# Down biases moved into the first block's product, one slot table on two column tiles, and constant matmuls in three router waits

## The chip, the cores and the metric

One core of a Trainium2 chip runs the whole kernel. The metric is the device time of one execution in microseconds (us); lower is better. The kernel before takes 1793.83 us (median of 3 runs, 1792.36 to 1794.33).

## What is computed

One inference step of a layer: an mLSTM branch and a latent-attention branch, merged, an output projection and a residual (x1), then an RMSNorm (x2) and a mixture of experts with top 4 of 32, then the final norm. Everything is float32. There are 336 tokens (64 of the sample stream, 272 of the prompt stream) of width 1024. Cut to what the change touches:

```python
logits = x2 @ w_router + b_router
top_v, top_i = lax.top_k(logits, TOP_K)
gates = softmax(top_v)
# sort (token, expert) pairs by expert, pad each expert's rows to whole blocks
ys = block of rows: hid @ w_dn[e] + b_dn[e],   hid = (up + 1) * gate * sigmoid(1.702 * gate)
x = x1 + sum over the token's experts of ys * gate
```

## The kernel before, in words

The kernel is written for each engine by hand: each engine has its own program, and they meet by semaphores. Eight PSUM banks are handed out in the order of a list of jobs (`job_list`, from L143): job n has bank n modulo 8, and `begin` (L578), `filled` and `taken` wait by that number.
**Up to the router.** Projections, attention and mLSTM run first. Then the output projection makes x1 in three row tiles (128, 128 and 80 tokens), each is normed into x2, transposed (`x2_turned`), copied by ScalarE and multiplied by the router's weights (`router`), and VectorE finds the top 4 (`choose`). `count(t)` (L895 to L902) counts the chosen experts with matmuls of constants.

**The tables.** VectorE works out for each of the 336 x 4 pairs a slot in padded blocks of 64 rows (BLK): the block `blkc` and the slot in it, `slotc`, for 12 columns of 128 rows. `inblk` (12 x 55, one-hot over the blocks) and `inslot` (12 x 64, one-hot over the slots) are factors of a matmul that scatters values into a table of 64 slots by 55 blocks. Two values are scattered: the token (`valc`, multiplied into the left half of `spread` by GpSimd at L1805) and the row of the result (`val4`: four times the token plus the turn, which of the token's up to four experts this is; right half, by VectorE). So job `tab` is 12 matmuls of 110 columns into partitions 0 to 63, and job `tab2` is the same 12 again into partitions 64 to 127, for the indices of the second half of each result row. VectorE reads `tab` with one operation (add and minimum) into `idxf`, casts it to `idx` (semaphore `idx_set`), and GpSimd gathers the 64 token rows of block 0 by it (`rows_in`, L1810). Before job `tab` TensorE waits for `tab_d` (VectorE, `inslot` and the right half of `spread`) and `tab_p` (GpSimd's half). `moe_tab` says that the tables of all engines are ready; PE then reads the number of blocks into a register.

**Down biases.** The sum over experts of gate times b_down is one matmul of K = 32: `gateT` (32 x tokens) by `bd_rows` (32 x 1024), six matmuls of 512 columns (`down_bias`, L934): two (tile t = 0, jobs `bd`) stand before the first block's tokens are transposed, four (t = 1, 2) behind the gate and up product of block 0. VectorE adds each to x1.

**Blocks.** For each of 39 blocks: 64 gathered rows are transposed (`tokens_turned`) and copied by ScalarE to `xg`; `bias` adds gate and up biases (L965); `gate_up(k)` for k = 0 to 7 (L975, and L981 for k = 7) multiplies with two column tiles of 64 (the halves of a bank), 1 MB of weights for each k; VectorE and ScalarE make `hid`; `hidden_turned`; `down(j)` (L998). Block 0's `gate_up` stands before the loop; the loop's pass b does the down product of block b and the `gate_up` of block b + 1. The order is: tokens, bias, hidden turn, gate_up(0), down(0), down(1), down(2), gate_up(1), down(3), gate_up(2) to (7).

**Weights.** The on-chip ring holds one expert's 12 MB (12 loads of 1 MB). SyncE (L545 to L553) reloads a slot for the next expert when TensorE has gone over it for the last block of the expert that was there: eight gate/up loads wait for `m_up`, then four down loads for `m_down`, one after another in its queue. Expert 0's weights are loaded before the router.

Of the kernel before, what the change touches and what calls it, by code (L numbers as in the profile page):

```python
# [18 lines left out]
ALU = mybir.AluOpType  # L19
# [7 lines left out]
NT = TS + TP  # L27
# [8 lines left out]
NB1 = MAXB + 2  # L36
# [8 lines left out]
for _name, _n in [("ident", 128), ("ones", 128), ("below", 128), ("cos", NT), ("sin", NT), ("swap", 64),  # L45
                  ("mask", NT), ("sel", 4 * 128), ("expert", NE), ("block", NB1), ("lane", 1),
                  ("slot", BLK), ("thr", 6), ("tok", 12), ("pad", 3), ("tok4", 12)]:
    CONST_AT[_name] = (_at, _n)
    _at += _n
# [3 lines left out]
def constants():  # L53
    c = np.zeros((128, CONST_N), np.float32)

    def put(name, a):
        o, n = CONST_AT[name]
        c[:a.shape[0], o:o + n] = a

    put("ident", np.eye(128))  # L60
    put("ones", np.ones((128, 128)))
    put("below", np.triu(np.ones((128, 128)), 1))
    half = ROPE // 2
    pos = np.concatenate([TM + PAST + np.arange(TS), np.arange(TP)]).astype(np.float32)
# [20 lines left out]
    put("tok", first + p - NT)  # L85
    put("tok4", TOPK * (first + p - NT))
    put("pad", np.concatenate([NT + p % BLK, 2 * (TOPK * NT + p % BLK) + p // BLK,
                               np.where(p % BLK, 2 * NT, NT - 1)], axis=1))
    return c
# [36 lines left out]
def job_list():  # L126
# [40 lines left out]
    j += [("pos",), ("cntT",), ("x2T", 2, 0), ("x2T", 2, 1), ("lg", 2), ("pend",), ("tab",), ("be",), ("gT",), ("tab2",)]  # L167
    j += [("bd", 0, s) for s in range(2)]
    return j
# [12 lines left out]
def build(nc, i, o, x_rows_dram, y_rows_dram):  # L182
    with ExitStack() as ctx:
# [39 lines left out]
        def r3(ap, a):  # L223
            return ap.rearrange("p (a b) -> p a b", a=a)
# [76 lines left out]
        posm = r3(small(3 * NE), 3)  # L301
        slotc, blkc, valc = small(12), small(12), small(12)
        nblkT, pendT = small(1, NE), small(1, NE)
# [19 lines left out]
        inblk = r3(r_kv[:, 1536:1536 + 12 * NB1], 12)  # L323
        spread = r3(r_o[:, 384:384 + 24 * NB1], 12)
        prod = r_o[:, 0:384].rearrange("p (t k e) -> p t k e", t=3, k=4)
# [41 lines left out]
        def taken(eng, *name):  # L367
# [26 lines left out]
        x_sent, yrow_free = sem("x_sent"), sem("yrow_free")  # L394
        nblkT_set, cmpT_set, gates_norm, inblk_set, tab_d, tab_p, idx_set, table_clear, be_set, idx_now = map(sem, (
            "nblkT_set", "cmpT_set", "gates_norm", "inblk_set", "tab_d", "tab_p", "idx_set", "table_clear", "be_set",
            "idx_now"))
# [182 lines left out]
        def _(pe):  # L580
# [6 lines left out]
            def end(ins, *name):  # L587
                ins.then_inc(bank_full[JOB[name] % 8], 1)
# [302 lines left out]
            def count(t):  # L891
# [11 lines left out]
                if t == 2:  # L903
                    end(ins, "cntT")

            count(0)
            x2_turned(2)
            router(2)
# [3 lines left out]
            b = begin("pend")  # L912
            end(group(b[0:NE, 0:1], [(cst("below")[0:NE, 0:NE], nblkT[:, :])]), "pend")
            pe.wait_ge(tab_d, 1)
            pe.wait_ge(tab_p, 1)
            pairs = [(inslot[0:m, 4 * t + k, :], spread[0:m, 4 * t + k, :]) for t, (_, m) in enumerate(ROWS)
                     for k in range(4)]
            b = begin("tab")
            end(group(b[0:BLK, 0:2 * NB1], pairs), "tab")
            pe.wait_ge(cmpT_set, 1)  # L920
# [6 lines left out]
            end(ins, "gT")  # L927
            b = begin("tab2")
            end(group(b[BLK:2 * BLK, 0:2 * NB1], pairs), "tab2")
            taken(pe, "gT")  # L930

            def down_bias(b, t, s):
                c0, m = ROWS[t]
                return pe.matmul(b[0:m, :], gateT[:, c0:c0 + m], bd_rows[:, 512 * s:512 * s + 512], start=True, stop=True)  # L934

            for s in range(2):
                b = begin("bd", 0, s)
                end(down_bias(b, 0, s), "bd", 0, s)

# [8 lines left out]
            pe.wait_ge(moe_tab, 1)  # L949
            for name in ("pos", "cntT", "pend", "be", "tab", "gT", "tab2"):  # L950
                taken(pe, name)
            for s in range(2):
                taken(pe, "bd", 0, s)
            nb = pe.value_load(nbi[0:1, 0:1].bitcast(I32), min_val=NE, max_val=MAXB)
            pe.wait_ge(m_xrow, 16)
            tokens_turned()
# [366 lines left out]
        def _(dve):  # L1323
# [302 lines left out]
            for t in range(3):  # L1626
# [23 lines left out]
            step(stt(slotc, blkc, -float(BLK), d12, ALU.mult, ALU.add))  # L1650
            step(tt(valc, cst("tok"), slotc, ALU.subtract))
            signal(tt(inblk, cst("block").unsqueeze(1).broadcast_to([128, 12, NB1]),
                      blkc.unsqueeze(2).broadcast_to([128, 12, NB1]), ALU.is_equal), inblk_set, 1)
            step(tt(later, dest.unsqueeze(3).broadcast_to([128, 3, 4, 4]), dest.unsqueeze(2).broadcast_to([128, 3, 4, 4]),
# [3 lines left out]
            step(tt(val4, val4, turn_of.rearrange("p t k -> p (t k)"), ALU.add))  # L1658
            step(tt(spread[:, :, NB1:2 * NB1], inblk, val4.unsqueeze(2).broadcast_to([128, 12, NB1]), ALU.mult))
            signal(tt(inslot, cst("slot").unsqueeze(1).broadcast_to([128, 12, BLK]),  # L1660
# [19 lines left out]
            signal(ts(pick, lane, be[:, 0:1], ALU.is_equal), m_pick, 1)  # L1680
            take(ts(idxf[0:BLK, 1, :], tab[0:BLK, NB1:2 * NB1], 2.0, ALU.mult, cst("pad", BLK)[:, 1:2], ALU.add), "tab")
            filled(dve, "tab2")
            take(ts(idxf[BLK:128, 1, :], bank(("tab2",))[BLK:128, NB1:2 * NB1], 2.0, ALU.mult,
                    cst("pad")[BLK:128, 1:2], ALU.add), "tab2")
            signal(dve.tensor_copy(idx[:, 1, :].bitcast(U32), idxf[:, 1, :]), idx_set, 2)
            for s in range(2):
                filled(dve, "bd", 0, s)
                x = x1[:, 0, 512 * s:512 * s + 512]
# [69 lines left out]
        def _(pool):  # L1758
# [46 lines left out]
            pool.tensor_tensor(spread[:, :, 0:NB1], inblk, valc.unsqueeze(2).broadcast_to([128, 12, NB1]), ALU.mult  # L1805
                               ).then_inc(tab_p, 1)

            def rows_in(column):
# [69 lines left out]
```

## Time and profile before

| what | us |
|---|---|
| median of 3 runs | 1793.83 |
| the profiled execution's own time | 1794.13 |
| its span | 1792.3 |
| TensorE busy | 1596.8 (89%) |
| VectorE busy | 363.6 (20%) |
| ScalarE busy | 372.3 (21%) |
| GpSimd busy | 122.1 (7%) |
| HBM read | 471.26 MB, 272 GB/s over the span |

The span is what the trace covers; about 1.8 us of the execution's own time lie outside it. Busy time of TensorE is modelled from its pipelined instructions. Times in rows are counted from the span's start. The router and its tables lie at about 640 to 698 us, block 0 begins at 698 us, and the blocks last to some 30 us before the end.

### The profile page before, as it was taken

Reading aid. Unit: us, or ns where it says so; the run is one execution under the profiler, and the core shown is the slowest. Engines: PE = TensorE matmul, PEld = TensorE weight load, DVE = VectorE, ACT = ScalarE, POOL = GpSimd, SP = SyncE. Lnnn points to the kernel's source line nnn. Section 1 sums busy time; section 2 is a strip of 40 time slices with the busy share of each in tenths; the row PEclk is TensorE's granted clock in tenths of the full one; section 3 lists DMA queues with packets and bytes.
Section 4 is the critical chain, followed back from the end, with each engine's and each line's share of the span. In section 5 each row is a group of like instructions: output and inputs, shape, how many; then the busy total and the mean of one; then the engine's idle time right before and its main releaser. Section 6 shows DMA issues by size and latency. Waiting matters only on the chain.

```text
span 1792.3 us, 20636 instructions
## 1 busy us (share of the span) xinstructions
PE 1596.8 (89%) x7124; PEld 732.7 (41%) x7125; DVE 363.6 (20%) x859; ACT 372.3 (21%) x724; POOL 122.1 (7%) x219
## 2 busy tenths in 40 slices
PE   6899999999999997988879998878899978899894
PEld 4565665666666643322223332222233322233231
DVE  3443442223231123110101101100111100111015
ACT  3443242353430020110101111101111101111111
POOL 0100000000000000100001010100011100011000
PEclk9989999899999997998989999989899989899997
DMA  7212112221209524899998999999999999849898
GB/s 251 69 47 74 47 48 94 72 71 47 95 1 303 187 99 175 347 409 413 413 405 324 401 354 413 411 409 407 362 363 360 405 409 406 351 179 406 339 403 283
DMA packets 108777, 477.36 MB, mean 266 GB/s; under 512 B 12995, under 2 KB 16944, under 8 KB 75970
## 3 DMA queue, kind: packets, MB, share of 16 engines
q1 hardware_dynamic: 100696, 461.77, 65.9%
q0 software_dynamic: 7808, 15.00, 2.5%
q8 instruction: 23, 0.38, 0.1%
q10 hardware_dynamic: 234, 0.08, 0.0%
q14 instruction: 16, 0.13, 0.0%
HBM read 471.26 MB, written 15.50 MB: 272 GB/s over the span
## 4 chain that ended last, share of the span: by engine, by line
PE 70%; DMA 17%; DVE 5%; issue 3%; SPq 2%; ACT 1%; DVEq 0%; ACTq 0%; POOL 0%; POOLq 0%
PE bank L592 30%; PE bank L975 20%; DMA ring<-in_w_gate_up 16%; PE bank L998 16%; PE bank L596 3%; PE bank L981 1%; DVE r_kv L1346 1%; DVE r_v L1349 1%; DMA b_router_b<-in_b_router 1%; SPq L546 0%; SPq L553 0%; SPq L462 0%; DVE r_c L1349 0%; DVE r_qk L1343 0%; DVE ring L1343 0%
## 5 line engine op out<-in xcount | busy, mean ns | idle before, releaser
L975 PE MATMUL bank<-ring,r_kv 128*64 128x512 f32 x2184 | 521.1, 625 | 95.6 <-DMA ring<-in_w_gate_up 95.6
L975 PEld LDWEIGHTS bank<-ring,r_kv 128*64 128x64 f32 x2184 | 157.1, 142 | 408.7 <-issue 309.0
L998 PE MATMUL bank<-ring,r_kv 128*64 128x512 f32 x1248 | 294.6, 616 | 0.7 <-ACT r_kv L1063 0.7
L592 PE MATMUL bank<-r_xt,ring 128*128 128x336 f32 x848 | 256.6, 458 | 1.8 <-DVE r_xt L1346 1.5
L1343 DVE TENSOR_SCALAR r_kv<-bank 128x512 f32<-128x512 f32 (+1 forms) x80 | 54.9, 687 | 930.5 <-PE bank L981 924.0
L592 PEld LDWEIGHTS bank<-r_xt,ring 128*128 128x128 f32 x848 | 161.7, 194 | 83.4 <-issue 13.2
L998 PEld LDWEIGHTS bank<-ring,r_kv 128*64 128x64 f32 x1248 | 93.8, 145 | 200.6 <-issue 199.7
L1063 ACT ACTIVATE r_xt<-bank 128x512 f32<-128x512 f32 x39 | 23.3, 597 | 521.6 <-PE bank L998 521.6
L592 PE MATMUL bank<-ring 128*128 128x336 f32 (+4 forms) x336 | 98.2, 435 | 4.1 <-DVE ring L1502 3.9
L1289 ACT ACTIVATE r_o<-r_kv 128x512 f32<-128x512 f32 x39 | 24.6, 632 | 324.7 <-DVE r_kv L1343 324.7
L596 PEld LDWEIGHTS bank<-const,r_v 64*128 64x128 f32 (+3 forms) x524 | 45.4, 139 | 79.4 <-DVE r_v L1349 44.5
L592 PEld LDWEIGHTS bank<-ring 128*128 128x128 f32 (+4 forms) x336 | 59.1, 184 | 39.5 <-issue 16.8
L592 PE MATMUL bank<-ring,r_kv 128*128 128x128 f32 (+6 forms) x256 | 72.5, 417 | 2.1 <-DVE r_kv L1346 1.2
L981 PE MATMUL bank<-ring,r_kv 128*64 128x512 f32 x312 | 73.5, 592 | 0.0
L596 PE MATMUL bank<-const,r_v 64*128 64x64 f32 (+3 forms) x524 | 61.8, 255 | 12.1 <-DVE r_v L1349 10.2
L1063 ACT ACTIVATE r_kv<-bank 128x512 f32<-128x512 f32 (+3 forms) x85 | 49.8, 586 | 80.8 <-PE bank L596 75.9
L592 PE MATMUL bank<-r_kv,ring 128*128 128x336 f32 (+10 forms) x240 | 59.5, 379 | 0.0
L965 PE MATMUL bank<-bgu,r_qk 32*64 32x512 f32 x312 | 44.2, 636 | 12.0 <-DVE r_kv L1343 12.0
L592 PEld LDWEIGHTS bank<-ring,r_kv 128*128 128x128 f32 (+4 forms) x256 | 40.1, 189 | 33.9 <-issue 24.7
L1289 ACT ACT_TABLE_LOAD x39 | 50.0, 1283 | 12.7 <-ACT r_xt L1063 12.6
L1834 POOL COPY r_qk<-r_qk 128x1 uint32 x39 | 7.0, 180 | 570.2 <-ACT r_xt L1063 570.2
L592 PEld LDWEIGHTS bank<-r_kv,ring 128*128 128x128 f32 (+3 forms) x240 | 35.5, 179 | 24.1 <-issue 14.3
(235 smaller groups left out, 988.2 us busy)
## 6 DMA issues: line engine op xcount, KB each, us to landing
ring<-in_w_gate_up SPq DMA_DIRECT2D x256, 1024.0 KB, 17.1
ring<-in_w_down SPq DMA_DIRECT2D x128, 1024.0 KB, 14.6
ring<-in_w_in SPq DMA_DIRECT2D x12, 2048.0 KB, 8.1
ring<-in_w_proj_b SPq DMA_DIRECT2D x2, 2048.0 KB, 8.8
ring<-in_w_proj_a SPq DMA_DIRECT2D x2, 2048.0 KB, 8.9
ring<-in_w_out SPq DMA_DIRECT2D x2, 2048.0 KB, 7.8
ring<-y_rows SPq DMA_DIRECT2D x8, 512.0 KB, 9.1
ring<-in_w_uq SPq DMA_DIRECT2D x2, 1152.0 KB, 9.0
```

The source lines that it names most:

```text
L592: ins = pe.matmul(out, l, r, start=(n == 0), stop=(n == len(pairs) - 1), **kw)
L596: return pe.transpose(out, src, ident[0:src.shape[0], 0:src.shape[0]])
L965: pe.matmul(half(gate_bank if q < 2 else up_bank, q % 2), pick[32 * q:32 * q + 32, :], bgu[32 * q:32 * q + 32, :], start=True, stop=False, ...
L975: ins = pe.matmul(half(gate_bank if q < 2 else up_bank, q % 2), xg[:, k, :], w[:, 512 * q:512 * q + 512], start=False, stop=False, skip_gr ...
L981: ins = pe.matmul(half(bank_, t), xg[:, 7, :], w[:, 512 * (q0 + t):512 * (q0 + t) + 512], start=False, stop=True, skip_group_check=True)
L998: ins = pe.matmul(half(out_bank, t), hidT[:, j, BLK * h:BLK * h + BLK], w[:, h, 512 * t:512 * t + 512], start=(j == 0 and h == 0), stop=(j ...
L1063: return act.activation(out, src, ACT.Copy, scale=scale)
L1289: act.activation(sg, gt, ACT.Sigmoid, scale=ALPHA).then_inc(m_sig, 1)
L1343: return dve.tensor_scalar(out, a, s1, s2, op0, op1)
L1346: return dve.tensor_tensor(out, a, b, op)
L1349: return dve.scalar_tensor_tensor(out=out, in0=a, scalar=s, in1=b, op0=op0, op1=op1)
L1834: pool.tensor_copy(now[:, 1:2].bitcast(U32), idx[:, 1, bass.ds(pool.snap(b), 1)].bitcast(U32)).then_inc(idx_now, 1)
```

## The change

- `count(0)` is followed by two matmuls of constants of 512 columns (`keep_going`), `pend` by five, and the read of the number of blocks by one. Their results are overwritten.
- One table in place of two: `spread` has 55 columns for each of 12, the token's half (`valc`, constant `tok`, GpSimd's multiply, semaphores `inblk_set` and `tab_p`) is gone. Job `tab` is now 12 x 2 matmuls of 55 columns, alternately into partitions 0 to 63 and 64 to 127; `tab2` is gone. The token is worked out from the combined value by two more `ts` operations (add, times 0.25; add, add a large constant; subtract it, minimum), and one operation makes the result rows of both halves.
- The two matmuls of jobs `bd` and their waits are gone from in front of block 0. All six down biases stand within block 0's `gate_up`: four before k = 2, two before k = 5 (these wait until VectorE has added the first two). The loop waits for all six.

```diff
-    j += [..., ("pend",), ("tab",), ("be",), ("gT",), ("tab2",)]
-    j += [("bd", 0, s) for s in range(2)]
+    j += [..., ("pend",), ("tab",), ("be",), ("gT",)]
...
+            def keep_going(b, n):
+                for _ in range(n):
+                    pe.matmul(b[:, :], ident, const[:, 0:512], start=True, stop=True, skip_group_check=True)
             count(0)
+            keep_going(begin("x2T", 2, 0), 2)
             x2_turned(2)
...
             end(group(b[0:NE, 0:1], [(cst("below")[0:NE, 0:NE], nblkT[:, :])]), "pend")
+            keep_going(begin("tab"), 5)
             pe.wait_ge(tab_d, 1)
-            pe.wait_ge(tab_p, 1)
...
-            end(group(b[0:BLK, 0:2 * NB1], pairs), "tab")
+            for n, (l, r) in enumerate(pairs):
+                for half_ in range(2):
+                    ins = pe.matmul(b[BLK * half_:BLK * half_ + BLK, 0:NB1], l, r, start=(n == 0), ...)
+            end(ins, "tab")
...
-            b = begin("tab2")
-            end(group(b[BLK:2 * BLK, 0:2 * NB1], pairs), "tab2")
...
-            for s in range(2):
-                b = begin("bd", 0, s)
-                end(down_bias(b, 0, s), "bd", 0, s)
...
             nb = pe.value_load(nbi[0:1, 0:1].bitcast(I32), min_val=NE, max_val=MAXB)
+            keep_going(xt_bank, 1)
             pe.wait_ge(m_xrow, 16)
             tokens_turned()
...
             for k in range(8):
+                if k == 2:
+                    for n in range(4):
+                        down_bias(banks[4 + n], n // 2, n % 2).then_inc(bd_full, 1)
+                if k == 5:
+                    pe.wait_ge(bd_free, 2)
+                    for n in range(4, 6):
+                        down_bias(banks[n], n // 2, n % 2).then_inc(bd_full, 1)
                 gate_up(k, 0)
-            for n, (t, s) in enumerate([(t, s) for t in (1, 2) for s in range(2)]):
-                down_bias(banks[4 + n], t, s).then_inc(bd_full, 1)
-            pe.wait_ge(bd_free, 1)
+            pe.wait_ge(bd_free, 6)
...
-            step(tt(valc, cst("tok"), slotc, ALU.subtract))
...
-            step(tt(spread[:, :, NB1:2 * NB1], inblk, val4..., ALU.mult))
+            step(tt(spread, inblk, val4..., ALU.mult))
...
-            step(ts(idxf[0:BLK, 0, :], tab[0:BLK, 0:NB1], cst("pad", BLK)[:, 0:1], ALU.add, cst("pad", BLK)[:, 2:3],
-                    ALU.min))
+            step(ts(idxf[0:BLK, 0, :], tab[0:BLK, 0:NB1], cst("pad", BLK)[:, 0:1], ALU.add, 0.25, ALU.mult))
+            step(ts(idxf[0:BLK, 0, :], idxf[0:BLK, 0, :], -0.375, ALU.add, 12582912.0, ALU.add))
+            step(ts(idxf[0:BLK, 0, :], idxf[0:BLK, 0, :], 12582912.0, ALU.subtract, cst("pad", BLK)[:, 2:3], ALU.min))
...
-            take(ts(idxf[0:BLK, 1, :], ...), "tab")
-            filled(dve, "tab2")
-            take(ts(idxf[BLK:128, 1, :], ...), "tab2")
+            take(ts(idxf[:, 1, :], tab[:, 0:NB1], 2.0, ALU.mult, cst("pad")[:, 1:2], ALU.add), "tab")
...
-            for s in range(2):
-                filled(dve, "bd", 0, s)
-                take(tt(x, bank(("bd", 0, s))[:, :], x, ALU.add), "bd", 0, s)
-            for n, (t, s) in enumerate([(t, s) for t in (1, 2) for s in range(2)]):
+            for n in range(6):
+                t, s = n // 2, n % 2
...
-                signal(tt(x, banks[4 + n][0:m, :], x, ALU.add), bd_free, n + 1)
+                signal(tt(x, banks[4 + n % 4][0:m, :], x, ALU.add), bd_free, n + 1)
...
-            pool.wait_ge(inblk_set, 1)
-            pool.tensor_tensor(spread[:, :, 0:NB1], inblk, valc..., ALU.mult).then_inc(tab_p, 1)
```

## Rows read from the trace of the kernel before

**Rows 1.** The page: busy tenths of the DMA engines, 40 slices of 44.8 us.

```profile
DMA  7212112221209524899998999999999999849898
```

**Rows 2.** Chain that ended last, whole run: start us, us, what.

```profile
760.61 16.46 DMA ring<-in_w_gate_up
```

**Rows 3.** DMA stretches: us, busy us of five engines, PEclk, DMA share, GB/s.

```profile
703.00:722.00 19.00, 15.42 (x70) 5.35 (x70) 5.49 (x12) 1.11 (x2) 1.14 (x2) 0.90 0.98 410
...
724.00:730.00 6.00, 6.00 (x28) 1.96 (x28) 0.00 (x0) 0.60 (x1) 0.00 (x0) 0.91 0.12 34
```

**Rows 4.** Timeline of SyncE's queue, block 0 and after: start us, us, what.

```profile
701.66 12.33 SPq L549 DMA_DIRECT2D ring<-in_w_gate_up  x8
728.51 7.24 SPq L553 DMA_DIRECT2D ring<-in_w_down  x4
```

**Rows 5.** Chain that ended last, 679 to 749 us: start us, us, what.

```profile
679.27 0.18 DVE r_qk L1346
...
680.84 0.91 DVE r_qk L1346
...
688.86 2.42 PE bank L592 x24
...
694.00 0.99 issue
694.99 1.10 PE bank L596 x8
696.09 1.91 PE bank L965 x8
698.00 13.76 PE bank L975 x56
711.76 1.72 PE bank L981 x8
713.48 3.64 PE bank L934 x8
...
724.39 2.22 PE bank L975 x8
...
743.77 0.89 PE bank L981 x4
...
748.34 1.87 PE bank L975 x8
```

**Rows 6.** Stretches of the router and block 0: columns as in rows 3.

```profile
667.00:687.50 20.50, 9.89 (x58) 9.25 (x59) 14.59 (x47) 3.05 (x9) 1.85 (x2) 0.50 0.47 184
...
695.00:701.00 6.00, 6.00 (x24) 2.21 (x26) 0.00 (x0) 1.88 (x2) 0.95 (x1) 0.50 0.08 25
```

**Rows 7.** Timeline of TensorE, 656 to 688 us, start first; brackets: idle before.

```profile
656.60 7.03 PE L592 MATMUL bank<-ring,r_kv 128*80 128x512 f32 x16
663.47 1.87 PE L592 MATMUL bank<-r_xt,r_o 128*128 128x32 f32 x16
...
667.87 1.33 PE L596 MATMUL bank<-const,r_qk 80*128 80x80 f32 x8 [1.89 <-DVE r_qk L1349]
669.83 2.31 PE L592 MATMUL bank<-r_xt,r_o 128*80 128x32 f32 x16 [0.63 <-ACT r_o L1063]
...
675.73 0.26 PE L592 MATMUL bank<-r_qk,const 32*32 32x1 f32 x2 [0.52 <-DVE r_qk L1636]
683.88 4.23 PE L592 MATMUL bank<-r_o,r_kv 128*64 128x110 f32 x24 [7.88 <-DVE r_kv L1346]
```

**Rows 8.** Timeline, an mLSTM chunk's scores: 64 weight columns, 64 moving columns.

```profile
417.05 1.15 PE L592 MATMUL bank<-r_qk 128*64 128x64 f32 x16
```

**Rows 9.** Timeline, VectorE's first table read and GpSimd's first gather.

```profile
688.22 0.33 DVE L1343 TENSOR_SCALAR r_qk<-bank,const 64x55 f32<-64x55 f32 x1 [1.92 <-PE bank L592]
...
689.70 1.04 POOL L1810 DMA_INDIRECT r_v<-x_rows,r_qk  x1 [7.98 <-DVE r_qk L1677]
```

**Rows 10.** DMA issues from 680 to 705 us: median us from issue to landing.

```profile
r_v<-x_rows,r_qk POOLq DMA_INDIRECT x2, 3.2
```

More of the change, by code:

```diff
@@ L46 @@
                   ("mask", NT), ("sel", 4 * 128), ("expert", NE), ("block", NB1), ("lane", 1),
-                  ("slot", BLK), ("thr", 6), ("tok", 12), ("pad", 3), ("tok4", 12)]:
+                  ("slot", BLK), ("thr", 6), ("pad", 3), ("tok4", 12)]:
     CONST_AT[_name] = (_at, _n)
@@ L84, in constants @@
     first = np.repeat([c0 for c0, _ in ROWS], TOPK)[None, :]
-    put("tok", first + p - NT)
     put("tok4", TOPK * (first + p - NT))
-    put("pad", np.concatenate([NT + p % BLK, 2 * (TOPK * NT + p % BLK) + p // BLK,
+    put("pad", np.concatenate([TOPK * NT + p % BLK, 2 * (TOPK * NT + p % BLK) + p // BLK,
                                np.where(p % BLK, 2 * NT, NT - 1)], axis=1))
@@ L166, in job_list @@
         j += [("lg", t - 1)] if t else []
-    j += [("pos",), ("cntT",), ("x2T", 2, 0), ("x2T", 2, 1), ("lg", 2), ("pend",), ("tab",), ("be",), ("gT",), ("tab2",)]
-    j += [("bd", 0, s) for s in range(2)]
+    j += [("pos",), ("cntT",), ("x2T", 2, 0), ("x2T", 2, 1), ("lg", 2), ("pend",), ("tab",), ("be",), ("gT",)]
     return j
@@ L301, in build @@
         posm = r3(small(3 * NE), 3)
-        slotc, blkc, valc = small(12), small(12), small(12)
+        slotc, blkc = small(12), small(12)
         nblkT, pendT = small(1, NE), small(1, NE)
@@ L323, in build @@
         inblk = r3(r_kv[:, 1536:1536 + 12 * NB1], 12)
-        spread = r3(r_o[:, 384:384 + 24 * NB1], 12)
+        spread = r3(r_o[:, 384:384 + 12 * NB1], 12)
         prod = r_o[:, 0:384].rearrange("p (t k e) -> p t k e", t=3, k=4)
@@ L394, in build @@
         x_sent, yrow_free = sem("x_sent"), sem("yrow_free")
-        nblkT_set, cmpT_set, gates_norm, inblk_set, tab_d, tab_p, idx_set, table_clear, be_set, idx_now = map(sem, (
-            "nblkT_set", "cmpT_set", "gates_norm", "inblk_set", "tab_d", "tab_p", "idx_set", "table_clear", "be_set",
+        nblkT_set, cmpT_set, gates_norm, tab_d, idx_set, table_clear, be_set, idx_now = map(sem, (
+            "nblkT_set", "cmpT_set", "gates_norm", "tab_d", "idx_set", "table_clear", "be_set",
             "idx_now"))
@@ L918, in _ @@
             b = begin("tab")
-            end(group(b[0:BLK, 0:2 * NB1], pairs), "tab")
+            for n, (l, r) in enumerate(pairs):
+                for half_ in range(2):
+                    ins = pe.matmul(b[BLK * half_:BLK * half_ + BLK, 0:NB1], l, r, start=(n == 0), stop=(n == len(pairs) - 1),
+                                    skip_group_check=True)
+            end(ins, "tab")
             pe.wait_ge(cmpT_set, 1)
@@ L949, in _ @@
             pe.wait_ge(moe_tab, 1)
-            for name in ("pos", "cntT", "pend", "be", "tab", "gT", "tab2"):
+            for name in ("pos", "cntT", "pend", "be", "tab", "gT"):
                 taken(pe, name)
-            for s in range(2):
-                taken(pe, "bd", 0, s)
             nb = pe.value_load(nbi[0:1, 0:1].bitcast(I32), min_val=NE, max_val=MAXB)
+            keep_going(xt_bank, 1)
             pe.wait_ge(m_xrow, 16)
@@ L1650, in _ @@
             step(stt(slotc, blkc, -float(BLK), d12, ALU.mult, ALU.add))
-            step(tt(valc, cst("tok"), slotc, ALU.subtract))
-            signal(tt(inblk, cst("block").unsqueeze(1).broadcast_to([128, 12, NB1]),
-                      blkc.unsqueeze(2).broadcast_to([128, 12, NB1]), ALU.is_equal), inblk_set, 1)
+            step(tt(inblk, cst("block").unsqueeze(1).broadcast_to([128, 12, NB1]),
+                    blkc.unsqueeze(2).broadcast_to([128, 12, NB1]), ALU.is_equal))
             step(tt(later, dest.unsqueeze(3).broadcast_to([128, 3, 4, 4]), dest.unsqueeze(2).broadcast_to([128, 3, 4, 4]),
@@ L1658, in _ @@
             step(tt(val4, val4, turn_of.rearrange("p t k -> p (t k)"), ALU.add))
-            step(tt(spread[:, :, NB1:2 * NB1], inblk, val4.unsqueeze(2).broadcast_to([128, 12, NB1]), ALU.mult))
+            step(tt(spread, inblk, val4.unsqueeze(2).broadcast_to([128, 12, NB1]), ALU.mult))
             signal(tt(inslot, cst("slot").unsqueeze(1).broadcast_to([128, 12, BLK]),
@@ L1680, in _ @@
             signal(ts(pick, lane, be[:, 0:1], ALU.is_equal), m_pick, 1)
-            take(ts(idxf[0:BLK, 1, :], tab[0:BLK, NB1:2 * NB1], 2.0, ALU.mult, cst("pad", BLK)[:, 1:2], ALU.add), "tab")
-            filled(dve, "tab2")
-            take(ts(idxf[BLK:128, 1, :], bank(("tab2",))[BLK:128, NB1:2 * NB1], 2.0, ALU.mult,
-                    cst("pad")[BLK:128, 1:2], ALU.add), "tab2")
+            take(ts(idxf[:, 1, :], tab[:, 0:NB1], 2.0, ALU.mult, cst("pad")[:, 1:2], ALU.add), "tab")
             signal(dve.tensor_copy(idx[:, 1, :].bitcast(U32), idxf[:, 1, :]), idx_set, 2)
-            for s in range(2):
-                filled(dve, "bd", 0, s)
-                x = x1[:, 0, 512 * s:512 * s + 512]
-                take(tt(x, bank(("bd", 0, s))[:, :], x, ALU.add), "bd", 0, s)
-            for n, (t, s) in enumerate([(t, s) for t in (1, 2) for s in range(2)]):
+            for n in range(6):
+                t, s = n // 2, n % 2
                 m = ROWS[t][1]
@@ L1802, in _ @@
                 pool.dma_start(x_rows_dram[c0:c0 + m, :], x2[0:m, t, :]).then_inc(x_sent, 16)
-            pool.wait_ge(inblk_set, 1)
-            pool.tensor_tensor(spread[:, :, 0:NB1], inblk, valc.unsqueeze(2).broadcast_to([128, 12, NB1]), ALU.mult
-                               ).then_inc(tab_p, 1)
             def rows_in(column):
```

## The prediction, made before the changed kernel ran

> **What bounds the kernel now.** I read the page's slices first: the DMA engines are at 8 to 9 tenths almost everywhere from slice 17 on [rows 1], so the expert blocks live near the weight stream. The chain that ended last agrees: from 760.61 us it runs through a 16.5 us gate/up weight load, the first of many, with stretches of TensorE between them [rows 2]. So what shortens a block's arithmetic is worth little; what lets block 0, and with it the whole stream, start earlier is worth its full size. That needs a second look at where the stream begins. Expert 1's gate/up loads are issued from 701.66 us, behind block 0's own gate_up, and the DMA engines are full (0.98, 410 GB/s) from 703 to 722; then they are nearly idle (0.12) from 724 to 730, because the down loads are issued only at 728.51, when block 0's first down product is done [rows 3, 4]. After that they stay busy. The event that starts the steady stream is therefore block 0's down product: what comes before it on TensorE's path, at 640 to 728 us, is what the end hangs on.
>
> The third view is that path in order of time [rows 5]. A row is start, duration, engine. The reader sees three costs. First, serial small steps of VectorE up to the tables. Second, TensorE at its lower clock level: the granted clock is 0.50 (1.2 GHz) from 667 to 687.5, after short matmuls with waits between them, and again from 695 to 701, after the wait of 1.80 us before the tokens [rows 6]. Third, a hole around block 0's end: four down biases (713.48), and the next gate_up only at 724.39, where in the following block it begins 2.85 us after the last one's end (743.77 plus 1.72, to 748.34) [rows 5].
>
> **The change, step by step.** Durations are of the profiled execution (1794.13 us, 0.30 above the median of 1793.83); gains are differences, so I take them off the median.
>
> 1. *Two constant matmuls after count(0).* A 512-column matmul at the full clock (2.4 GHz) takes 0.86 us (8 of them from 656.60 to 663.47), so two take 1.72 and fit in the idle 1.89 before the transposes of tile 2 [rows 7]: cost 0, at most 0.2 if the clock drops within. If they hold the clock, the third router product costs 1.87 in place of 2.31 and the transposes about 0.2 less [rows 7]. I take 0.65 gained; bounds 0.2 lost, 1.0 gained (counts warm too).
>
> 2. *One table's VectorE work.* The 0.18 at 679.27 (`valc`) goes. The operation at 680.84 lasts 0.91 for the same 12 columns, while GpSimd multiplies [rows 5]; with GpSimd's operation gone it should be 0.18, so 0.73 more. Gain 0.9. GpSimd was not itself waited for; it is idle afterwards, and nothing else is late in its queue.
>
> 3. *Five constant matmuls after pend.* By 1 they start about 0.65 earlier than 676.0 [rows 7], at 675.35. At the full clock they take 4.3 us, at half 8.6. `tab_d` comes at 683.88 less 0.65 less 0.9, that is 682.3. They end between 679.65 and 683.95; with a rise of the clock midway, 682. Cost: I take 0.1, bounds 0 and 1.6.
>
> 4. *The table.* Before, the 24 instructions of 110 columns took 4.23 us, mostly at half clock, and tab2's 24 took 2.42 at full clock, 0.101 each [rows 5, 7]. Now 48 instructions of 55 columns. The nearest row is the score product (64 weight columns, 64 moving): 16 in about 1.1, 0.068 each [rows 8], so 48 take 3.2 without overlap. Bounds: 24 x 0.068 = 1.6 (halves entirely side by side) and 48 x 0.101 = 4.8. I take 2.9 and the full clock: gain 1.3. Column tiles do overlap here for 512 columns: 8 instructions of gate_up take 1.72 us, 0.215 each, where the 128-row form takes 0.43 [rows 5, 7]. The Trainium skill (TensorE: Matmul & The Clock Gate, Part 3: Packing small matmuls) says that matmuls whose outputs lie in different column groups run concurrently; by it alone the table would take 1.6 and the gain would be 1.3 more. tab2's 2.42 us lay ahead of the down biases, and goes with them.
>
> 5. *Index work.* Two more VectorE operations before the gather, at most 0.33 each (the PSUM form) [rows 9]; without PSUM I take 0.25 each: cost 0.5. Both sit before the cast that GpSimd waits for.
>    So the table ends at 688.1 - 0.65 - 0.9 + 0.1 - 1.3 = 685.35, and the gather, issued 1.6 behind it before (689.70), is issued 2.1 behind it: 687.45, and lands 3.0 later (median 3.2 of two issues, one under load [rows 10]): 690.5.
>
> 6. *What PE does meanwhile.* It waits for `moe_tab` and for VectorE to free the table: the ops from 688.22 on take about 2.4 with the added ones, so 687.8; 0.99 of issue and register read [rows 5]; then one constant matmul, 0.86 to 1.71: 689.7 to 690.5. It is ready as the gather lands; cost 0, at most 0.3. The tokens' transposes begin at 690.5 in place of 694.99: **gain 4.5** (steps 1 to 5 give 2.25; the other 2.25 are the two down biases and their VectorE adds, which held the bank and the register read although the gather had landed near 692.7).
>
> 7. *Clock at block 0.* Before, PE was at half clock up to 701.2; seven gate_ups took 13.76 in place of 7 x 1.72 = 12.04 [rows 5, 6], 1.7 lost. Now PE is busy without a gap from 688.8, some 6 us sooner, against a block start 4.5 sooner: about 0.4 of cold is left. **Gain 1.3**; bounds 0 and 3 (the transposes' 1.10 and the biases' 1.91 were cold too).
>
> 8. *Down biases in block 0.* Six at 0.86 are 5.16. They are K = 32 by 128 columns amid products of 128 by 64. Four of them took 3.64 us, 0.20 over 4 x 0.86, with one change of form [rows 5]; four changes now make some 0.45. So +5.6; the 3.64 at the end go. The hole: from 717.12 to 724.39 is 7.27, since VectorE first had to do four adds, three gate operations and a register read before it took gate and up. All that is now done during the product, so the hole is the next block's 2.85 [rows 5]. 5.6 - 3.64 - 4.42: **gain 2.5**. The next gate_up took 2.22 partly cold, 1.87 warm: **0.35**. The wait for two adds before k = 5 is covered: 0.7 us adds against three gate_ups. Refill: k = 2 to 7 free their slots later, so expert 1's loads stall about 2 us before k = 2 and end at about 719.6; the down loads are issued at 719.9. No loss, but the slack is thin.
>
> Sum: 4.5 + 1.3 + 2.5 + 0.35 = 8.65 us at block 0's first down product, carried to the end because the stream from there on is shifted as a whole. 1793.83 - 8.65 = **1785.2 us** (the profiled execution 1785.5).
>
> **Rivals.** (a) *More*: the halves overlap and the clock holds throughout: table 1.3 more, clock 1.7 more: 1782.2. For it, gate_up's overlap. Against it, the gaps of 2 us and more that still lie between the short matmuls. (b) *The constants do not hold the clock*, or the 48 instructions cost 0.101 each: 1.3 + 0.65 of clock and 1.9 of table go, and up to 1.5 for a late step 3; some of it: about 1788.7 (1787 to 1790.2). For it: two warm matmuls followed by a router of 32-column products, of the kind behind which the clock fell at 667. (c) *The gain does not reach the end*: expert 1's gate/up loads, held up by the moved biases, end at 719.6 against about 723 before, only 3.4 earlier; if the stream hangs on these, 1793.83 - 3.4 = 1790.4, and with a late table 1792. For it: the row of a nearly full DMA up to 722. Against it: the idle 6 us after it. (d) *Slower*: changing the tile costs time. The place is the table (47 changes of column tile) and block 0 (4 changes of form). At 0.23 us a change they cost 51 x 0.23 = 11.7 and the time is 8.65 less that, 1796.9; it decides from 0.17 us a change. Against it: gate_up changes the column tile at every second instruction and shows nothing, and the one change of form in the trace costs 0.20 with four matmuls around it [rows 5]. The Trainium skill (TensorEngine Tiling, Key Properties) says that a change of tiling mode drains TensorE, and a change of tile alone does not; by that rule block 0's four changes would cost and the table's 47 would not, which leaves this rival about 1 us and the forecast as it is. The trace's 0.20 agrees.
> That the change does not do what it says is (b).
>
> **Numbers.** About 0.2% (3.6 us) can be told from no change; 1790.2 is the bound. Forecast 0.56, (a) 0.12, (b) 0.15, (c) 0.13, (d) 0.04. Faster is forecast, (a) and (b): 0.83. Same is (c): 0.13. Slower is (d): 0.04. The range: down to (a) with 0.7 of spread between runs, 1781.5; up through (b) to 1789.7, leaving out (c) and (d).
>
> **What would show it.** Right: the table at 2.5 to 3.3 us for 48 instructions; the gather issued near 687.5; transposes near 690.5; block 0's gate_up (with six down biases) from about 693.5, its down product 8 to 9 us earlier; down loads of expert 1 issued near 720; the hole behind block 0 at about 3 us. Wrong, step by step: a granted clock of 0.5 through the first gate_ups (7); the table start after 683 (3); the down loads shifted by 8 but the end by 3 (c); table over 4.8 us (d).

## The result and the profile after

The changed kernel takes 1781.34 us (median of 4 executions, 1779.35 to 1782.65) against 1793.09 for the kernel before in the same rounds (4 executions): ratio 0.9932, 95% interval 0.9916 to 0.9948. It is 11.75 us faster where 8.65 was forecast, and lies 0.16 us under the range's lower end of 1781.5. The profiled execution took 1780.27 us with a span of 1778.4. One execution of all that follow, a slow one of the kernel with the biases alone (1922.31 us, granted clock 0.82 against 0.93 to 0.94 in the others of that kernel), stands in no comparison.

The chain of the kernel after, in order of time, from the first constants to the next block; start, duration, what. It answers to [rows 5].

```profile
665.76 1.91 PE bank L907 x4
...
669.25 1.32 PE bank L590 x16
...
685.45 2.88 DMA r_v<-x_rows,r_qk
...
688.37 1.11 PE bank L594 x8
689.49 1.91 PE bank L965 x8
691.40 4.96 PE bank L975 x16
696.36 3.62 PE bank L940 x8
699.98 5.30 PE bank L975 x24
705.28 1.87 PE bank L940 x4
707.15 3.58 PE bank L975 x16
710.74 0.88 PE bank L981 x4
...
715.29 1.87 PE bank L975 x8
717.16 5.15 PE bank L998 x24
```

The timeline of the same kernel, for what [rows 7] and [rows 9] showed of before:

```profile
674.06 6.03 PE L907 MATMUL bank<-const 128*128 128x512 f32 x10
...
681.09 1.61 PE L925 MATMUL bank<-r_o,r_kv 128*64 128x55 f32 x48 [0.99 <-DVE r_kv L1351]
...
682.63 0.42 PE L590 MATMUL bank<-r_qk,const 32*128 32x55 f32 x2
...
683.37 0.14 DVE L1673 CAST r_qk<-r_qk 1x1 int32<-1x1 f32 x1
...
683.54 0.27 DVE L1348 TENSOR_SCALAR r_qk<-bank,const 64x55 f32<-64x55 f32 x1
...
685.45 1.01 POOL L1805 DMA_INDIRECT r_v<-x_rows,r_qk  x1 [17.02 <-DVE r_qk L1682]
...
686.73 1.53 PE L907 MATMUL bank<-const 128*128 128x512 f32 x2 [3.28 <-issue]
```

Stretches of TensorE in it (us, busy us, granted clock, DMA share, GB/s), against [rows 6]:

```profile
667.00:673.90 6.90, 4.16 (x39) 0.98 1.01 382
...
683.40:686.70 3.30, 0.04 (x1) 1.00 0.00 0
686.70:688.40 1.70, 1.55 (x3) 0.68 0.22 65
688.40:694.70 6.30, 6.30 (x26) 0.54 0.08 23
694.70:700.00 5.30, 5.30 (x18) 1.00 0.76 260
```

And SyncE's queue: first down loads of expert 1, and the last loads before the end, against [rows 4]:

```profile
719.06 7.24 SPq L551 DMA_DIRECT2D ring<-in_w_down  x4
...
1742.77 19.87 SPq L563 DMA_DIRECT2D ring<-y_rows  x12
```

The reader sees four things. The clock stays full through the third router product (0.98) and the 48 table instructions take 1.54 us (681.09 to 682.63), but then VectorE is what is late: it reads the table only at 683.54, 0.91 behind its end, after its own small operations. TensorE stands idle for 3.28 us before the single constant; the clock falls behind that idle stretch, during the constant (0.68), and block 0 begins at half clock (0.54), as before. Block 0's first down product begins at 717.16 (before: 724.39 + 2.22 = 726.61), 9.45 us earlier, 0.23 of which was there already before the router. The profiled executions lie further apart than that, 1794.13 to 1780.27, or 13.86: the first down load is issued 9.45 us earlier and the last loads 13.76 earlier (the kernel before issues these at 1756.53):

```profile
1756.53 20.01 SPq L565 DMA_DIRECT2D ring<-y_rows  x12
```

So the loop was 4.3 us shorter in this one execution (1023.7 in place of 1028.0 us), with nothing in it changed. Whether that belongs to the change was the first question for the experiments. In what follows the distance from the first `count` matmul to the first down load is used: 63.34 us in the kernel before, 54.12 after, so 9.2 gained.

### The profile page after: what moved, and what is told of

The parts are those of the page before. It is cut to its first block, busy times and chain, and to the rows that moved or that the text cites. A ratio compares the mean times of both kernels' runs of the same rounds, so it can differ in the third digit from the quotient of the medians.

```text
span 1778.4 us, 20662 instructions
## 1 busy us (share of the span) xinstructions
PE 1592.5 (90%) x7140; PEld 727.7 (41%) x7141; DVE 363.0 (20%) x859; ACT 372.7 (21%) x724; POOL 121.2 (7%) x218
## 4 chain that ended last, share of the span: by engine, by line
PE 71%; DMA 17%; DVE 6%; issue 3%; SPq 1%; ACT 1%; DVEq 0%; POOLq 0%; POOL 0%; ACTq 0%
PE bank L590 30%; PE bank L975 20%; DMA ring<-in_w_gate_up 16%; PE bank L998 16%; PE bank L594 3%; PE bank L981 1%; DVE r_kv L1351 1%; DVE r_v L1354 1%; DVE ring L1348 0%; SPq L544 0%; SPq L551 0%; DMA ring<-in_x_prompt 0%; DVE r_qk L1348 0%; DVE r_c L1354 0%; PE bank L940 0%
## 5 line engine op out<-in xcount | busy, mean ns | idle before, releaser
L590 PEld LDWEIGHTS bank<-ring 128*128 128x128 f32 (+4 forms) x336 | 58.1, 181 | 38.7 <-issue 15.5
L594 PE MATMUL bank<-const,r_v 64*128 64x64 f32 (+3 forms) x524 | 61.4, 253 | 10.5 <-DVE r_v L1354 10.4
```

Source lines behind the costliest of these rows:

```text
L590: ins = pe.matmul(out, l, r, start=(n == 0), stop=(n == len(pairs) - 1), **kw)
L594: return pe.transpose(out, src, ident[0:src.shape[0], 0:src.shape[0]])
```

## Experiments

**The down biases alone.** On the kernel before:

```diff
-            for s in range(2):
-                b = begin("bd", 0, s)
-                end(down_bias(b, 0, s), "bd", 0, s)
...
+                if k == 2:
+                    for n in range(4): down_bias(...)
+                if k == 5:
+                    pe.wait_ge(bd_free, 2)
+                    for n in range(4, 6): down_bias(...)
...
```

> The kernel before with only the down biases moved (none before block 0, four before k = 2 and two before k = 5 of its gate_up). Theory (the steps' prices hold and the shift is carried to the end): the gather had landed near 692.7, so the tokens' transposes begin 2.0 to 2.3 us earlier (about 692.8), block 0's stretch from the first gate_up to the next is 2.2 to 2.7 shorter, the first down product begins 4.5 to 5 us earlier than 726.61, and the median falls by 4 to 6 us. Rival (the later slots of the ring set the end): median within 2 us of before. Rival (changes of the tile's form drain the array): the six biases take over 7 us together.

Its timeline:

```profile
689.74 1.04 POOL L1805 DMA_INDIRECT r_v<-x_rows,r_qk  x1 [8.01 <-DVE r_qk L1675]
...
692.73 0.70 PE L595 MATMUL bank<-const,r_v 64*128 64x64 f32 x8 [1.42 <-DMA r_v<-x_rows,r_qk]
693.36 1.09 PE L958 MATMUL bank<-bgu,r_qk 32*64 32x512 f32 x8
```

The transposes now begin when the gather lands, at 692.73, as forecast. The distance to the first down load is 57.24 us, 6.1 less, of which 1.3 is luck with the clock (transposes and bias at full clock, 1.65 us in place of 2.94). The six biases take 5.5 us. The median of nine executions is 1788.85 against 1792.08 (27 executions), 3.2 us; the ratio, 0.9994 with 0.9975 to 1.0012, can't be told from no change. So the 4 to 6 us expected at the end are not shown, although the profiled execution itself was 5.9 us shorter than that of before. The difference is not explained; the nine executions range over 10.5 us.

**No constants.** `keep_going` emits nothing.

```diff
-                for _ in range(n):
+                for _ in range(0):
```

> The changed kernel without any of its eight constant matmuls; what is computed is the same. Theory (the first two hold the clock through the third router product, the five hold it for the table, the last one buys nothing because the clock fell before it): the clock falls after count(0) as before, the router product takes 2.2 to 2.4 in place of 1.32, the count and table follow at half clock, the table's 48 instructions take 3.0 to 3.3 in place of 1.61, and the gather is issued 2.5 to 3.5 us later than in the changed kernel (its read no longer waits for VectorE); block 0's own stretch is unchanged within 0.5. Median 2 to 4 us above the changed kernel. Rival (the clock would have held anyway or the constants cost what they give): within 1 us.

```profile
669.30 2.31 PE L590 MATMUL bank<-r_xt,r_o 128*80 128x32 f32 x16 [0.63 <-ACT r_o L1068]
...
682.45 2.81 PE L925 MATMUL bank<-r_o,r_kv 128*64 128x55 f32 x48 [6.99 <-issue]
...
697.18 3.70 PE L940 MATMUL bank<-r_v,r_o 32*128 32x512 f32 x8
700.81 7.01 PE L975 MATMUL bank<-ring,r_kv 128*64 128x512 f32 x24
```

The router product is back at 2.31 and the table at 2.81 us, both at half clock (the table a little cheaper than the 3.0 expected), and the distance to the first gather rises from 20.51 to 22.66 us, 2.15 later, less than the 2.5 to 3.5 expected. To the first down load it is 56.98 (54.12 with the constants): they are worth 2.9 us there. Median 1786.46, ratio 0.9970 (0.9956 to 0.9983) to before. The first two and the five together did their work; no kernel left out only one of the groups, so how the gain divides between them is not shown. A surprise is the last row: 24 gate/up instructions behind the four biases took 7.01 us, where the changed kernel took 5.37 in the same view.

**A delay of known size.**

```diff
             pe.wait_ge(m_xrow, 16)
+            keep_going(xt_bank, 8)
             tokens_turned()
```

> The changed kernel with eight more constant matmuls between the landing of the gather and the transposes of block 0's tokens. They take 8 to 11 us there, and the clock is full when block 0 begins, which gives back 2.5 to 3: the first down product comes 5 to 8 us later than in the changed kernel. Theory (all after it is shifted as a whole): the median is later by the shift of the profile's first down product, within 2 us. Rival (part of the start's gain is lost or enlarged later): the end moves by less than two thirds or by more than four thirds of it.

```profile
686.85 9.87 PE L907 MATMUL bank<-const 128*128 128x512 f32 x18 [3.24 <-issue]
```

The distance to the first down load is 59.56, 5.4 more than in the changed kernel (with block 0 at full clock, the 16 instructions in 3.65 us). The median is 1787.97, ratio 0.9981 (0.9963 to 0.9998) to before: 4.1 us gained where the distance says 3.8. Against all executions of the changed kernel (1782.65, below) it is 5.3 later, where the distance says 5.4. What starts later ends later by as much, as far as medians can tell: the interval is 6 us wide.

**The table's halves in turn.**

```diff
-            for n, (l, r) in enumerate(pairs):
-                for half_ in range(2):
+            for half_ in range(2):
+                for n, (l, r) in enumerate(pairs):
```

> The changed kernel with the table's 24 matmuls in another order: twelve for partitions 0 to 63, then twelve for 64 to 127. Theory (adjacent matmuls on different column tiles run side by side): without neighbours the 48 instructions take 3.0 to 3.3 us (0.068 each, as in the score product) in place of 1.61, but VectorE is late to read the table by 0.9, so the gather is issued only 0.6 to 0.9 us later; median within 1.5 us of the changed kernel. Rival (55 columns are simply cheap, 0.034 each in any order): 1.6 us again.

```profile
674.94 2.82 PE L925 MATMUL bank<-r_o,r_kv 128*64 128x55 f32 x48 [0.95 <-DVE r_kv L1351]
...
681.01 1.88 PE L907 MATMUL bank<-const 128*128 128x512 f32 x2 [2.51 <-issue]
...
683.87 1.44 PE L965 MATMUL bank<-bgu,r_qk 32*64 32x512 f32 x8
...
685.25 3.65 PE L975 MATMUL bank<-ring,r_kv 128*64 128x512 f32 x16
```

and TensorE's stretch behind the idle one (us, busy us, granted clock, DMA share, GB/s):

```profile
681.00:683.87 2.87, 2.85 (x10) 0.54 0.15 39
```

(This execution's router lies 6 us earlier in its span; only distances are compared.) The same 48 instructions take 2.75 us (2.82 less the last one's tail) in place of 1.54: neighbours on different column tiles run side by side (whether it is the matmuls or the weight loads of one tile beside the other's matmul, this doesn't separate). In turn, each costs 0.057, below the 0.068 of the score product [rows 8] and so below the 3.0 to 3.3 us expected. The gather is issued 0.46 us later. Yet the distance to the first down load is 52.80, 1.3 *less*: TensorE's idle stretch became 2.5 us in place of 3.3, and the clock, which fell behind it here too (0.54), was full again when block 0's gate_ups began (16 instructions in 3.65). Median 1781.12 against 1792.08, ratio 0.9937 (0.9917 to 0.9957). That pointed to the idle stretch.

**The changed kernel again, twice,** on two chips.

> The changed kernel again, unaltered, on the chip of the next three. Theory (the gain is 9 to 10 us up to block 0's first down product, and what the clock does before block 0 and in the waits for weights adds or takes some us, differently in each execution): median 9 to 12 us below the kernel before; from the third count to the first gate_up the same times within 0.1, except where the granted clock differs. Rival (the loop itself became shorter): from the first down product to the last loads, it is again 4 us shorter than in the kernel before.

> The changed kernel a third time, for the spread. Theory (9.2 us gained up to the first down load, and the loop as long as before): median 8 to 11 us below the kernel before; expert 1's first down load 54.1 us behind the first count at half clock before block 0, up to 2.9 less where the clock holds. Rival (11.75 us, as first measured, is its gain): median 11 to 13 us below.

SyncE's queue in the first of the two, then in the second:

```profile
720.94 7.24 SPq L551 DMA_DIRECT2D ring<-in_w_down  x4
...
1748.05 20.36 SPq L563 DMA_DIRECT2D ring<-y_rows  x12
```

```profile
718.22 7.24 SPq L551 DMA_DIRECT2D ring<-in_w_down  x4
...
1745.02 20.65 SPq L563 DMA_DIRECT2D ring<-y_rows  x12
```

The distance to the first down load is 54.10 and 54.14 us, the same to 0.04, while the loop takes 1027.1 and 1026.8 us, close to the 1028.0 of before. The shorter loop of the first profile does not come from the change. The length of the loop varies from execution to execution: 1023.7 to 1028.0 us over the fourteen profiles of all kernels, and 1027.1 and 1023.8 in two of one and the same kernel (wait filled and VectorE's order, below).

Medians: 1783.01 against 1791.85 (ratio 0.9946, 0.9931 to 0.9961; 8.8 us, just under the 9 to 12 expected) and 1782.71 against 1791.00 (0.9946, 0.9925 to 0.9967). Over all 17 executions of the changed kernel the median is 1782.65, over 54 of the kernel before 1792.08: **9.4 us gained**, beside the trace's 9.2.

**The idle stretch filled.**

```diff
             end(ins, "gT")
+            taken(pe, "cntT")
+            keep_going(bank(("cntT",)), 3)
             taken(pe, "gT")
```

> The changed kernel with three more constant matmuls, in the idle stretch between the gate transposes and the wait for the tables (their result is overwritten). Theory (block 0 began at half clock because TensorE stood idle for 3.3 us there): the clock stays full, the tokens' transposes, the bias and the first 16 gate/up instructions take 0.7, 0.9 to 1.1 and 3.4 to 3.65 in place of 1.11, 1.98 and 5.03, the first down product comes 2.5 to 3 us earlier relative to the gather's issue, and the median is 1 to 3 us below the changed kernel's. Rival (it was the waits after the register read): the clock still falls.

```profile
688.56 0.71 PE L594 MATMUL bank<-const,r_v 64*128 64x64 f32 x8 [0.70 <-DMA r_v<-x_rows,r_qk]
689.20 1.09 PE L967 MATMUL bank<-bgu,r_qk 32*64 32x512 f32 x8
690.21 3.65 PE L977 MATMUL bank<-ring,r_kv 128*64 128x512 f32 x16
693.80 3.69 PE L942 MATMUL bank<-r_v,r_o 32*128 32x512 f32 x8
697.42 7.07 PE L977 MATMUL bank<-ring,r_kv 128*64 128x512 f32 x24
```

and its stretches (us, busy us, granted clock):

```profile
686.00:690.00 4.00, 2.67 (x19) 1.00 0.10 28
693.80:697.40 3.60, 3.60 (x10) 1.00 0.88 355
697.40:701.00 3.60, 3.60 (x11) 0.53 0.50 205
```

Tokens, bias and the first gate_ups run at full clock, as expected. In all five profiles of kernels with the wait filled, block 0's first gate_ups ran at full clock; in all four profiles of the changed kernel, with and without its third constant, 16 instructions took 5.03 to 5.07. But the distance to the first down load falls by 0.85 only (53.27), not by 2.5 to 3, since the clock drops right behind the four down biases: TensorE was busy for 3.60 of 3.60 us there. Median 1781.90, ratio 0.9942 (0.9928 to 0.9955).

**VectorE's order as well.** In the kernel with the wait filled, the three operations on the block numbers go behind the cast that the gather waits for.

> The kernel of the filled wait, and VectorE's three small operations on the block numbers (0.56 us) behind the cast of the gather's indices instead of ahead of the table's read. Theory (VectorE, not the table, now ends last before the gather): the gather is issued 0.5 to 0.6 us earlier after the table's start (3.8 in place of 4.36), the tokens' transposes likewise unless TensorE is late from its constants; median 0 to 1 us below the filled wait alone. Rival (GpSimd or TensorE's register read ends last): nothing moves.

> The kernel of the filled wait and VectorE's order again, beside the changed kernel on one chip. Theory: table start, gather and tokens at the same distances from the first count as in its first profile (16.14, 19.91, 22.80 us); expert 1's first down load 50.8 us behind the first count, or up to 52.6 where the clock falls behind the four biases; median 1 to 4 us below the changed kernel's. Rival (its lower median was the spread between runs): less than 1 us below.

In the first of the two:

```profile
695.11 5.37 PE L977 MATMUL bank<-ring,r_kv 128*64 128x512 f32 x24
```

The gather is issued 19.91 and 19.93 us behind the first count in place of 20.51, and the first down load 50.81 and 50.85, 3.3 less than in the changed kernel; in both profiles the clock held behind the biases (24 instructions in 5.37 us), which alone is 1.7 of the 2.4 us by which they lie below the filled wait. The tokens came 0.7 earlier, which is the order's part. So the median lies 2.7 below the filled wait's, where 0 to 1 was expected. Medians 1779.17 (ratio 0.9926, 0.9907 to 0.9946) and 1779.35 (0.9933, 0.9910 to 0.9956). On the same chips the changed kernel had 1783.01 and 1782.71: this version is 3.8 and 3.4 us below it by the medians, though the intervals against the kernel before overlap. Its two medians are the lowest of all that ran.

**Without the third constant.** The line `keep_going(xt_bank, 1)` is left out.

> The changed kernel without the one constant matmul before the gather's wait. Theory (the clock has fallen before it; it only fills part of a wait): the tokens' transposes begin at the same time after the gather's issue (2.9 us), and the clock rises later in block 0, so that block 0's first gate/up stretch is 0 to 1 us longer. One time, within the spread of the changed kernel's. Rival (it holds the clock): block 0 is over 1.5 us longer.

Gather, transposes, first gate_ups and first down load lie at 20.51, 23.45, 26.41 and 54.15 us behind the first count, as in the changed kernel (20.51, 23.43, 26.39, 54.12). The third constant is worth nothing. Its one time was 1785.20.

**More down biases in a row.** To see whether the biases themselves let the clock go, the four before k = 2 are computed twice, in the kernel with the wait filled and VectorE's order.

```diff
+                    for n in range(4):
+                        down_bias(banks[4 + n], n // 2, n % 2)
                     for n in range(4):
                         down_bias(banks[4 + n], n // 2, n % 2).then_inc(bd_full, 1)
```

> The same kernel with four and two, and the four biases before k = 2 computed twice over (the first results are overwritten by equal ones), eight K = 32 matmuls in a row. Theory (such a run does not keep the clock): the granted clock falls to 0.5 within or right behind the eight, so that they and the next 24 gate/up instructions take 1.7 us or more over 6.9 + 5.2 = 12.1 us. Rival (TensorE fully busy holds the clock, and the falls seen came from the waits before block 0): 12.1 to 12.5 us and a clock of 1.0 throughout.

Its timeline, then its stretches:

```profile
692.90 9.74 PE L942 MATMUL bank<-r_v,r_o 32*128 32x512 f32 x16
702.56 7.80 PE L977 MATMUL bank<-ring,r_kv 128*64 128x512 f32 x24
```

```profile
694.00:696.00 2.00, 2.00 (x6) 1.00 1.02 422
...
698.00:700.00 2.00, 2.00 (x4) 0.50 0.12 49
```

Expected were 12.1 us for the two if the clock held; they took 17.4. The clock fell in the middle of the run, with TensorE busy all the time. In the delay kernel nine constants of 128 rows took 9.87 us in a row and ended at full clock (1.00 from 692.00 to 696.60, 4.60 of 4.60 us busy); eight biases of 32 rows began at full clock and ended at half. That points to these matmuls themselves. What in them it is, the 32 rows or the values they multiply, is not separated. The weight loads ran during the first half of them (DMA share 1.02) and not during the constants, but with the biases apart, below, they ran at 0.88 to 0.94 and the clock held. The one time was 1788.64.

**The biases apart,** in the same kernel.

```diff
-                if k == 2: ... four ...
-                if k == 5: ... two ...
+                if 1 <= k <= 6:
+                    n = k - 1
+                    if n == 4:
+                        pe.wait_ge(bd_free, 2)
+                    down_bias(banks[4 + n % 4], n // 2, n % 2).then_inc(bd_full, 1)
```

> The kernel of the filled wait and VectorE's order, with the six down biases one by one before k = 1 to 6 of block 0's gate_up in place of four and two together. Theory (a run of K = 32 matmuls can let the clock fall although TensorE is fully busy, as behind the four biases in the filled-wait kernel and in the one without constants; one between two gate_ups cannot): the granted clock stays at 1.0 through block 0, whatever the alignment; from the first gate_up to the first load of expert 1's down weights is 26.3 to 27.3 us (each change of form may add 0.05 to 0.2, twelve of them in place of four). Median within 2 us of the kernel with four and two. Rival (the fall had another cause): the clock falls again behind a bias in this or a like kernel.

```profile
686.26 1.94 PE L977 MATMUL bank<-ring,r_kv 128*64 128x512 f32 x8
688.13 1.12 PE L942 MATMUL bank<-r_v,r_o 32*128 32x512 f32 x2
```

The clock stays full through block 0, but eight more changes of form cost 1.35 us (the first down load at 52.20 in place of 50.85), 0.17 each; from the first gate_up it is 27.7 us, over the 26.3 to 27.3 expected. Median 1780.80, ratio 0.9939 (0.9915 to 0.9962); beside 1779.35 for four and two. Whether it is safer over many executions than four and two can't be told from one profile each.

The distances and the medians, side by side (us; gains against the kernel before, each on its own chip):

| kernel | to first down load | gained there | gained by the medians |
|---|---|---|---|
| before | 63.34 | | |
| changed (three times) | 54.12, 54.10, 54.14 | 9.2 | 11.75, 8.8, 8.3 |
| biases only | 57.24 | 6.1 | 3.2 |
| no constants | 56.98 | 6.4 | 5.6 |
| delay | 59.56 | 3.8 | 4.1 |
| halves in turn | 52.80 | 10.5 | 11.0 |
| filled wait | 53.27 | 10.1 | 10.0 |
| filled wait and order (twice) | 50.81, 50.85 | 12.5 | 12.7, 11.7 |
| biases apart | 52.20 | 11.1 | 10.2 |

Within 1 us, but for the first profile's kernel and the biases alone, what is gained up to the first down load is gained at the end.

## Why the prediction was right and wrong

**The bound: right.** Block 0's first down product sets when the weight stream runs steadily, and its shift is carried to the end, as the delay and the table of distances show; the biases alone are the exception, unexplained. Rival (c) is out: expert 1's gate/up loads did wait before k = 2 (their issue stretched over 18.12 us, 12.33 before), and nothing came of it.

**The range: wrong.** It ended 0.16 us above the measured median. The forecast was 1785.2; the 3.84 us between the two are made up of three parts. The three executions of before that I had (1793.83) lay 1.75 over the median of 54 (1792.08). The four of the changed kernel lay 1.31 under the median of 17 (1782.65). And the change gains 9.43 where the sum had 8.65: 0.78. The step that failed is the last of the numbers, the 0.7 us that I allowed for the spread between runs: single executions of the kernel before range over 15.8 us and medians of four to seven of the changed kernel over 1.7. In the first two traces the loop alone differed by 4.3 us. The lower end was rival (a)'s 1782.2 less that 0.7; the median of the 17, 1782.65, lies inside the range. What put 1781.34 outside is the spread, and not the mechanism.

**The sum, term by term** (by the profiles, 0.23 that lay before the router taken off):
- Step 1, first two constants: 0.65 forecast, 1.6 measured where VectorE compares the counts. The third router product took 1.32 us, not 1.87: I had taken the price of a product with 128 weight columns for one with 80, and the last counts ran at full clock too. Mis-sized.
- Step 2: 0.9 forecast, 0.94 measured. Step 3: the five constants ended at 680.1, 0.99 before `tab_d`; cost 0. Right.
- Step 4, the table: 2.9 us forecast, 1.54 measured, a little under the lower bound of 1.6. The step mis-sized is the overlap of the two column tiles, which I took as slight; the Trainium skill's rule (TensorE: Matmul & The Clock Gate, Part 3: Packing small matmuls) gave 1.6, and the trace agrees with its 1.54; the halves in turn show that it is the overlap. But of the 2.6 us gained only some 1.9 reached the gather, since VectorE read the table 0.9 behind its end (0.2 before). I had left that engine's order out.
- Step 5: 0.5 forecast, 0.43 measured; issue to landing 2.88 (3.0). So the gather is issued 4.0 us earlier, where steps 1 to 5 had 2.25. Step 6: from its issue to the tokens 2.4 us less than before, 2.25 forecast. Tokens: 4.5 us earlier forecast, 6.4 measured.
- Step 7, the clock at block 0: 1.3 forecast, nothing measured: the eight gate_ups together took 15.6 us, 15.5 before. The first 16 gate/up instructions took 4.96 us, in all four profiles of that part of the kernel 5.03 to 5.07 by the timeline, against 3.65 at full clock. I had TensorE busy from 688.8 on and did not count the 3.3 idle before that, behind which the clock fell. Filling them gave it back. The step's own figures also leave more cold than it says: with TensorE busy 6.2 us sooner and block 0 4.5 sooner, 1.5 of the 3.2 us at half clock remain and cost 0.75 us, not 0.4.
- Step 8: 2.5 forecast, 2.6 measured; six biases 5.49 (5.6), hole 2.83 (2.85). The gate_up behind it: 0.35 forecast and measured. Right.

So 1.9 us more than forecast up to the tokens and 1.3 us less in steps 7 and 8 nearly cancel, and that is luck: 9.2 against 8.65.

**The rivals.** (a) was half right: the halves overlap, the clock did not hold throughout; the version with the wait filled and VectorE's order, in which it did, is what (a) described. (b) is refuted by the kernel without constants for the first seven constants taken together, and holds for the eighth. (d) is out: 47 changes of column tile cost nothing measurable, and a change of form 0.17 each.

## What to carry to other kernels

Look for the event that starts the steady stream, measure variants by the distance of two events around the changed part in one trace, and use the median only to see that the distance is carried: here the distance repeated within 0.04 us and medians within 2. When a step is shortened, write down what every other engine still has to do at that point, because the next wait is often an engine that was hidden (VectorE here). Matmuls of constants pay where they bridge a wait right in front of work that is on the path, and one that comes only behind the idle stretch bought nothing here (54.15 us without it, 54.12 with it).

## What the runs showed of the hardware that was not expected

- TensorE can be busy without a gap and still lose its clock: behind or within a run of K = 32, 128-column matmuls the granted clock went from 1.0 to 0.5, with 3.60 of 3.60 us busy before it in one kernel, and in the middle of eight such matmuls in another, while a run of nine constants with 128 rows rose from half clock and ended at full clock. With four in a row before k = 2 it fell in two of eleven profiles.
- Adjacent matmuls of 55 columns on the two column tiles cost 0.032 us an instruction, and 0.057 when the tiles are not alternated, both at full clock (1.54 and 2.75 us for 48).
- Executions of the kernel before differ by up to 15.8 us in 1790. Over the fourteen profiles, the first count, with the same work ahead of it in all kernels, comes at 658.8 to 666.8 us, and the loop of blocks takes 1023.7 to 1028.0. So the larger part of the variation that the profiles show lies ahead of the changed part, and the distance between two events leaves it out. Why these parts vary was not settled by an experiment.
